# Modulation columns split into four spreads, memory rows turned at the stage border, exponentials issued ahead of the next high part

## The reference

```python
for l in range(DEPTH):                                   # DEPTH = 2
    mod = (cond @ w_mod[l] + b_mod[l])[:, None, :]       # 1024 -> 6 x 1024
    sh_a, sc_a, g_a, sh_f, sc_f, g_f = jnp.split(mod, 6, axis=-1)
    h = rms_norm(x, norm_mix[l]) * (1 + sc_a) + sh_a
    proj = h @ w_in[l]                                   # 1024 x 3072
    # 8 heads of softmax attention, 4 pairs of heads whose weights are a0 - lam * a1
    x = x + g_a * (jnp.concatenate([o_m, o_d], axis=-1) @ w_out[l])
    h = rms_norm(x, norm_ffn[l]) * (1 + sc_f) + sh_f
    x = x + g_f * ((jax.nn.silu(h @ w_gate[l]) * (h @ w_up[l])) @ w_down[l])
```

## Time and profile before

| what | value |
|---|---|
| median of 3 runs | 2824.2 us (2821.93 to 2825.02) |
| the profiled execution, its own time | 2823.45 us |
| its span, first to last instruction | 2821.7 us |
| PE busy | 2741.2 us (97%) |
| DVE busy | 2107.9 us (75%) |
| ACT busy | 1391.6 us (49%) |
| DMA | 537 MB, mean 190 GB/s |
| mean granted TensorE clock | 0.991 |

### The profile page before, as it was taken

How to read it: one execution, slowest core, us unless ns; L and a number is a source line. 1 busy time by engine, 2 the same in 40 slices (tenths; PEclk the granted TensorE clock), 3 DMA queues, 4 the chain that set the end, 5 groups by cost and what they waited for, 6 DMA issues and landing times.

```text
span 2821.7 us, 39962 instructions
## 1 busy us (share of the span) xinstructions
PE 2741.2 (97%) x16410; PEld 2339.2 (83%) x16410; DVE 2107.9 (75%) x3118; ACT 1391.6 (49%) x1630; POOL 208.1 (7%) x172
## 2 busy tenths in 40 slices
PE   8989998999999999999999999999999999999998
PEld 7768887788888788888888888897888888888887
DVE  7777865765555579999879955546699988799655
ACT  4545445554456455554444344465555544444443
POOL 0200001000013001110000000030011100000000
PEclk9999999999999999999999999999999999999999
DMA  8757853655553355554455555633455554454554
GB/s 331 285 216 280 317 187 134 217 194 193 194 200 135 134 179 180 194 179 166 165 176 187 174 194 194 229 135 134 166 178 194 181 174 169 164 194 168 192 194 142
DMA packets 75637, 537.41 MB, mean 190 GB/s; under 512 B 8512, under 2 KB 8896, under 8 KB 12096
## 3 DMA queue, kind: packets, MB, share of 16 engines
q1 hardware_dynamic: 75456, 534.86, 54.1%
HBM read 527.48 MB, written 7.34 MB: 190 GB/s over the span
## 4 chain that ended last, share of the span: by engine, by line
PE 65%; issue 22%; DVE 7%; ACT 4%; DMA 1%; POOL 1%; SPq 0%; DVEq 0%; POOLq 0%; ACTq 0%
PE banks L447 18%; PE banks L455 9%; PE banks L525 7%; PE banks L527 7%; PE banks L535 7%; DVE wlo L1524 3%; PE banks L499 3%; PE banks L501 2%; PE banks L510 2%; ACT whi L1019 2%; PE banks L469 1%; PE banks L471 1%; PE banks L481 1%; PE banks L964 1%; DMA raw<-in_win 1%
## 5 line engine op out<-in xcount | busy, mean ns | idle before, releaser
L1019 ACT ACTIVATE whi<-raw 128x2048 fp32r<-128x2048 f32 x438 | 838.8, 1916 | 990.4 <-issue 799.2
L1524 DVE TENSOR_TENSOR wlo<-raw,whi 128x2048 fp32r<-128x2048 f32 x438 | 1011.9, 2311 | 306.7 <-ACT whi L1019 306.4
L447 PE MATMUL banks<-ht,whi 128*128 128x512 f32 x2880 | 703.1, 393 | 5.9 <-DVE big L1609 2.9
L447 PEld LDWEIGHTS banks<-ht,whi 128*128 128x128 f32 x2880 | 526.5, 188 | 110.1 <-issue 3.7
L525 PE MATMUL banks<-whi,ht 128*128 128x512 f32 x1152 | 456.9, 397 | 13.0 <-DVE ht L1599 9.0
L527 PE MATMUL banks<-whi,ht 128*128 128x512 f32 x1152 | 450.4, 391 | 0.0
L455 PEld LDWEIGHTS banks<-ht,wlo 128*128 128x128 f32 x2880 | 369.1, 191 | 14.6
L455 PE MATMUL banks<-ht,wlo 128*128 128x256 f32 x2880 | 373.4, 283 | 0.0
L535 PE MATMUL banks<-wlo,ht 128*128 128x512 f32 x1152 | 287.4, 389 | 0.0
L525 PEld LDWEIGHTS banks<-whi,ht 128*128 128x128 f32 x1152 | 217.0, 188 | 58.4 <-issue 14.6
L535 PEld LDWEIGHTS banks<-wlo,ht 128*128 128x128 f32 x1152 | 216.2, 188 | 44.9
(11 more groups left out here) (279 smaller groups left out, 3357.5 us busy)
## 6 DMA issues: line engine op xcount, KB each, us to landing
raw<-in_pu SPq DMA_DIRECT2D x128, 1024.0 KB, 4.9
raw<-in_pv SPq DMA_DIRECT2D x128, 1024.0 KB, 4.9
raw<-in_win SPq DMA_DIRECT2D x52, 1024.0 KB, 4.9
big<-in_wmod SPq DMA_DIRECT2D x24, 1024.0 KB, 6.4
raw<-in_wmod SPq DMA_DIRECT2D x24, 1024.0 KB, 5.2
raw<-in_wgate SPq DMA_DIRECT2D x22, 1024.0 KB, 4.9
raw<-in_wup SPq DMA_DIRECT2D x22, 1024.0 KB, 5.1
raw<-in_wdown SPq DMA_DIRECT2D x22, 1024.0 KB, 4.9
```

The source lines that it names most:

```text
L447: m = e.matmul(bank[b + n], h[:, q, c[n]], M.both[:, q * 512:(q + 1) * 512], start=q == 0, stop=False, skip_group_check=True)
L1019: e.activation(whi(j), slot[u][0], ACT.Copy).then_inc(*hi.mark(j))
L1524: e.tensor_tensor(wlo(j), slot[u][0], whi(j).bitcast(F32), ALU.subtract).then_inc(*lo.mark(j))
```

## The change

1. The third chunk of the modulation's columns (parts `sc_f` and `g_f`) is cut in two: `(l, 2)` is `sc_f`, `(l, 3)` is `g_f`. A unit of them still has 1 MB, but holds two groups of 128 rows by 1024 columns, and VectorE works through it in two instructions of 1024 columns, the second behind a wait for the first. Four units make a part.
2. The orders in `lists`: mixer 0 now has twelve modulation units instead of sixteen, never two in a row; `(0, 3)`'s four move to the side slots in feed-forward 0, which then has twenty; mixer 1 keeps eight and starts them earlier.
3. `gate_row` leaves the borders of the stages: gate 0 of layer 1 moves from ahead of mixer 1 to its output projection (where layer 0 already has it), gate 1 of both layers moves from ahead of the feed-forward to after its gate and up units of i = 7.
4. In mixer 1 the four turns of the memory rows move from after unit 4 to ahead of the stage, in the place of `gate_row` and `warm`. ScalarE and VectorE take them over in the steps 0 to 2, two at a time.
5. In ScalarE's loop of both mixers `take` moves behind `score`. `head_squares` moves from step 14 to 13, and `head_sums` of step 14 moves ahead of VectorE's `take`.

```diff
     def munits(l, c):
-        return [("m", a["wmod"][l, c, k], l, c, k) for k in range(8)]
+        return [("m", a["wmod"][l, c, k], l, c, k) for k in range(8)] if c < 2 else [
+            ("m", a["wmod2"][l, c - 2, j], l, c, j) for j in range(4)]
...
-    units += first_mixer(0, [0, 1, 3, 4, 6, 7, 9, 10, 11, 12, 12, 13, 13, 14, 14, 15], munits(0, 1) + munits(0, 2))
-    units += ffn[0][0:1] + spread(ffn[0][1:], munits(1, 0) + munits(1, 1))
-    units += first_mixer(1, [3, 8, 11, 12, 13, 14, 15, 21], munits(1, 2)) + ffn[1]
+    units += first_mixer(0, [0, 1, 2, 3, 5, 7, 9, 11, 13, 15, 16, 17], munits(0, 1) + munits(0, 2))
+    units += ffn[0][0:1] + spread(ffn[0][1:], munits(0, 3) + munits(1, 0) + munits(1, 1))
+    units += first_mixer(1, [1, 4, 7, 10, 13, 16, 18, 20], munits(1, 2) + munits(1, 3)) + ffn[1]
...
# TensorE, first_mixer(1): the start, and after unit 4
-                gate_row(1, 0, (0, 1))
-                warm(name, 6)
+                for t in range(2):
+                    on.wait_ge(*d_mem[t].at(l))
+                for q in range(4):
+                    turn(("m", l), q, MEM, DG[1], q)
                 turn_all(name, XA, DG[0])
...
-                if l and j == 4:
-                    for t in range(2):
-                        on.wait_ge(*d_mem[t].at(l))
-                    for q in range(4):
-                        turn(("m", l), q, MEM, DG[1], q)
...
# TensorE, project and feed_forward
-                    if stage == ("mix1", 0):
-                        gate_row(0, 0, (4, 5))
+                    if stage[0] == "mix1":
+                        gate_row(stage[1], 0, (4, 5))
...
-            gate_row(l, 1, (0, 1))
             warm(name, 6)
...
+                if i == 7:
+                    b = banks.where["g", l, i]
+                    gate_row(l, 1, (b, b + 1))
...
# ScalarE, first_mixer
             for j in range(last + 1):
-                k = take()
                 if 8 <= j < 12:
                     score(2 * (j - 8))
                     score(2 * (j - 8) + 1)
                 if 12 <= j < 16:
                     score(j - 4)
-                if l and j == 5:
-                    for q in range(4):
+                k = take()
+                if l and j < 2:
+                    for q in (2 * j, 2 * j + 1):
                         turn_scaled(("m", l, q), COLS[:, l * 64 + 48:l * 64 + 56], MT, since)
...
-                if j == 14:
+                if j == 13:
                     head_squares(("o1", l, 0), [o[:, 0:512] for o in os], [TMP[:, 0:512], TMP[:, 512:1024]],
...
# VectorE, modulate
+            part(MACC[l, c], r[:, 0:1024], 2 * k, (l, c, k, "first"))
+            on.wait_ge(*mac.at((l, c, k, "first")))
+            part(MACC[l, c], r[:, 1024:2048], 2 * k + 1, (l, c, k))
...
# VectorE, first_mixer
+                if j == 14:
+                    head_sums(("o1", l, 0), [TMP[:, 0:512], TMP[:, 512:1024]], 8, 64, 168)
                 take()
...
-                if l and j == 5:
-                    for q in range(4):
+                if l and j in (1, 2):
+                    for q in (2 * j - 2, 2 * j - 1):
                         rest(("m", l, q), COLS[:, l * 64 + 48:l * 64 + 56], MT)
...
                 if j == 14:
-                    head_sums(("o1", l, 0), [TMP[:, 0:512], TMP[:, 512:1024]], 8, 64, 168)
                     head_scale(("o1", l, 0), [o[:, 0:512] for o in os], 8, 64, 168)
```

53 lines of the change are left out of this document (31 added, 22 removed).

## The result

The changed kernel takes **2816.36 us** in the median of 7 runs (2812.43 to 2820.18), the kernel before 2825.02 in the same comparison (2821.93 to 2826.01). The ratio is 0.9973 with a 95% interval of 0.9961 to 0.9985: faster, by 8.7 us between the medians. The forecast was 2808, that is 16.2 us under the median of before that it went by (2824.2). Nearly half of that gain did not come.

What follows compares the result with a forecast made beforehand. TensorE bounds feed-forward 0, so the gain lies in its waits in the mixers: -8.5 (mixer 0) - 14.4 (mixer 1) + 5.1 (gate rows) + 1.6 (starts) = -16.2 us, giving 2808 us, range 2802 to 2813; 2801 to 2819 with rivals.

Steps and rivals of the forecast that it cites:

- the step on the loop between VectorE and ScalarE: Both mixers: a turn of 7.0 us against TensorE's 8.1 holds TensorE only behind rope; 2.8 us and 1.2 + 1.2.
- what the order was good for: Mixer 0: waits of 15.0 us go, among them exponentials 4.5 and query copy 3.9, with slow stretches of 4.2.
- The memory rows: Mixer 1: turning 3.73 us leaves the path; the 7.27 us wait and a 2.5 us slow stretch go, -13.5.
- The gate rows: Three of them leave idle time for busy time, 1.71 us each, +5.1 us in all.
- The low parts in feed-forward 0: Four more modulation units there add 10 us to VectorE's 164.8 in 214; TensorE stays the bound.
- The halved units: Modulation in two instructions of 1024 columns: at most 0.3 us more per unit, 4 us in all, nothing on the path.
- The wait at win 3: Start of mixer 0: a load taking 7.2 us makes the high part late and TensorE waits 2.1 us.
- The end of mixer 0: Last combine and turned heads 3.2 us, a copy 0.5, projection units 0.4 and 1.7: 5.8, bounds 0 and 8.
- The feed-forward starts: At two starts the wait grows from about 1.0 to 2.7 us; the clock may fall, 1.6 taken, bounds 0 and 3.2.
- The rivals: Waits return, 2819 (0.17); better, 2801 to 2804 (0.10); ScalarE bound, 2834 (0.05); mixer 0 waits stay, 2821 (0.06).
- (a): Rival: the high part behind the exponentials is late in every step, mixer 0 gains nothing net; 2819 us, chance 0.17.
- (c): Rival: ScalarE becomes the bound, each of sixteen steps holds TensorE 1.97 us, +31.5; 2834 us, chance 0.05.

Runs made afterwards that it cites:

- e2: The changed kernel with the high part ahead of the exponentials in every step again, as in the kernel before; 2803.28 us, ratio 0.9920.
- e3: The kernel before with ScalarE's new order alone, head_squares and head_sums moved earlier too, nothing spread or moved besides; 2829.19 us, ratio 1.0012.

## Why the prediction was wrong, step by step

**What failed: the step on the loop between VectorE and ScalarE.** The prediction saw the loop (maxima, exponentials, high part, low part, next maxima) and let it cost nothing as long as its turn of 7.0 us was under TensorE's 8.1. It charged the new order 2.8 us in mixer 0, for a late copy of turned weights and a late query copy in steps 10 and 11, and 2.4 in mixer 1. Neither copy made TensorE wait there: in the changed kernel it has no wait from 124.14 to 170.19, nor from 488.33 to 543.75. What came instead was the wait of unit 10 for banks 2 and 3 in both mixers, and the order cost 13.1 us (2816.36 against 2803.28), 7.9 more than the 5.2 charged; the medians fall short of the forecast by 7.5. Without the 5.2 the sum is -21.4, and the run without the new order gives -22.3.

Two things are wrong in that step.

First, the comparison. In the kernel before the high part was made while ScalarE had nothing else to do, and the low part stood in VectorE's idle time. The turn had not existed so far, and it fits into TensorE's step only if it starts as soon as the scores are there. With the sums behind the low part of step 8, which the prediction did count (7.0 and 1.4 against 8.1), it was already too long, and the exponentials of step 9 came at 117.24, where the version with the high part first has them at 114.48.

Second, the list of what stands behind the high part on ScalarE. The prediction followed the copies of turned weights and the query copy, and not `projected`, which stands right behind them in the same queue and has to empty banks 2 and 3 for the next unit. In the kernel before ScalarE idled 1.31 us ahead of that copy, the copy ended at 123.95 and TensorE started unit 10 at 124.10. So the queue could take some 1.5 us more ahead of the copy before TensorE would feel it, and the high part alone is 1.92; no row of TensorE's waits shows such a slack.

Its price in the changed kernel, by stage and against e2: 3.7 us in mixer 0 (2.45 from unit 9 to unit 10, the rest at the end of the stage), 8.1 in mixer 1 (2.6 from unit 9 to unit 10, 4.4 by slow matmuls in unit 10, 1.15 in the late steps). That the waits themselves (2.54 and 2.70 us) are near the forecast 2.8 and 2.4 is luck, since they stand at another place for another cause; the 4.4 us of slow matmuls were not in the forecast at all.

**Also wrong: what the order was good for.** I gave it the 4.5 us of exponentials in mixer 0 and part of the query copy and the turned weights. The spreading alone takes these of mixer 0 away but for 0.6 us of the weights' copy. "Why the exponentials come late shows on ScalarE" was read rightly from the earlier trace rows (a late load, then a high part, then the exponentials), and then the change was credited with both cures for one illness, one of which has a price.

**Right in size.** The memory rows: 13.5 forecast, 13.4 measured. The gate rows: 1.71 each forecast, 1.74 in feed-forward 0 and 1.71 in the projection of mixer 1 measured. The low parts in feed-forward 0 stay hidden. The halved units: two instructions of 1284 ns are 2.57 against 2.35, 0.22 for the forecast of at most 0.3 (the first figure behind the bar is the busy time, the second the mean ns of one):

```profile
L1555 DVE SCALAR_TENSOR_TENSOR big<-raw,small,big 128x1024 f32<-128x1024 f32 x21 | 27.0, 1284 | 0.4
```

**Right in place, wrong in size.** The wait at win 3 came, with 0.94 us instead of 2.1 in this execution and 0.5 to 1.9 in the other kernels with this order. The load took longer than the row that I used, though, not the usual 4.9:

```profile
DMA to landing us min/median/max: 7.8/7.9/8.1
```

These are the two loads behind the scratch write here, against 7.2 before; TensorE itself came later, after a fall of the clock. The 4.4 us estimated for the megabyte from the Trainium skill (DMA: Bandwidth & Descriptors, Anatomy of one DMA) are further off still. The Trainium skill gives that fit for DMAs that GpSimd issues; in this trace SyncE issues the loads.

The end of mixer 0 was put at 5.8 with a bound of 8. The five waits there sum to 8.4, above that bound:

```profile
175.21 0.49 PE L654 MATMUL banks<-big 128*128 128x128 f32 x2 [0.34 <-ACT big L1150]
179.72 0.52 PE L642 MATMUL banks<-small,big 128*128 128x128 f32 x3 [3.15 <-DVE ht L1614]
180.81 0.79 PE L654 MATMUL banks<-big 128*128 128x128 f32 x2 [0.57 <-ACT big L1150]
193.43 2.11 PE L538 MATMUL banks<-wlo,ht 128*128 128x512 f32 x8 [1.26 <-DVE wlo L1526]
201.18 0.77 PE L528 MATMUL banks<-whi,ht 128*128 128x512 f32 x1 [3.04 <-ACT whi L1021]
```

The second had been put at 3.2 and the last at 1.7. The last is the third projection unit's slot, freed late by the last modulation units, 1.3 us more than forecast.

The feed-forward starts: the wait grew from 1.0 to 2.7 as forecast. A fall makes the turning 5.47 us long instead of 3.84 and the start 1.5 us longer, and it came at both, where I had put 1.6 for the two together.

**The signs.** Of the signs that the prediction named, these came: no wait behind the memory rows and full clock in the step after them, no wait of ScalarE's high part for a wkv load above 3 us in mixer 0, 2.7 us of idle time at the starts. The wait at win 3 is half of what it should be, and TensorE's waits in mixer 0, from its first matmul to 208 us, sum to 12.1 where 10 were expected; 2.54 of them are the wait that was not foreseen. The shortfall of 2.6 us in mixer 0 adds up so: the wait of unit 10 took 0.3 less than the 2.8 charged and win 3 1.2 less than forecast, the fall of the clock at the first unit 1.6 more, and the end of the stage 2.6 more, of which 1.2 are the new order's by the comparison above. The 2.9 in mixer 1 are 5.7 more for the order (8.1 against 2.4), less the 1.6 of the clock at the first unit and less 1.3 for an end of the stage that won more than forecast.

**The rest of the span.** Of the 6.8 us there, 1.7 are the gate row and 1.5 the start of feed-forward 1; the others are falls of the clock in the second stack, which the change does not touch: four in this execution, one in that of before, about 1.2 us each. They follow waits that both kernels have. At the same place, the changed kernel first:

```profile
1432.04 0.47 PE L528 MATMUL banks<-whi,ht 128*128 128x512 f32 x1 [2.00 <-DVE ht L1619]
```

```profile
1433.00:1436.40 3.40, 3.40 (x9) 2.67 (x9) 3.40 (x9) 0.16 (x1) 0.00 (x0) 0.50 0.00 0
```

and the kernel before, 9.8 us later, after the same 2.00 us of idle time:

```profile
1441.87 0.47 PE L525 MATMUL banks<-whi,ht 128*128 128x512 f32 x1 [2.00 <-DVE ht L1604]
```

```profile
1442.00:1446.00 4.00, 4.00 (x18) 3.29 (x19) 4.00 (x10) 0.78 (x2) 0.00 (x0) 1.00 0.00 0
```

So the profiled execution makes the shortfall look larger (10.6 us) than the medians do (16.2 less 8.7, that is 7.5).

**The rivals.** None of the four is what happened. (a) gave a time near the measured one (2819, by high parts that are late in every step), by luck, since its reason does not hold: TensorE waited for a bank in one step of each mixer. (c), ScalarE as the bound, has the right engine; its condition, a turn plus the work between above 8.1 us in most steps, was met in one step of each mixer (9), not in most. What was missing is a rival in which a copy out of PSUM, last in ScalarE's queue, holds a bank.

## What to carry to other kernels

Before moving an instruction back in an engine's queue, list everything that now comes later because of it, down to the last instruction of the step, and for each its slack: the idle time ahead of it in its own queue, and the time from its end to the start of whoever needs it. Here these were 1.31 and 0.15 us against 1.92 put ahead, and the second is in no list of waits. Where two edits cure the same wait, price each as if the other were already made: here the second cost 13 us. Look at which of the two removes the cause (the late load) before paying for the one that works around it.

## What the runs showed of the hardware that I had not expected

A wait of 2.7 us is not followed by half clock each time, and the same wait in the same program can go either way: at the start of mixer 1 every trace has the wait of 2.48 us of the earlier trace rows, and in 8 of 13 the clock fell behind it, in 5 not. Behind the shortest such waits of a start (1.0 us or less) it never fell. What decides between the two for 2.0 to 2.7 us is open. The runs of one kernel differ by 3 to 8 us, which would be two to five falls of 1.5 us; that falls make this scatter is not shown fall by fall, but the run of 2812.43 us of the changed kernel has a mean granted clock of 0.993, and those of 2819.87 and 2820.18 have 0.989.

A wait's length does not tell how long the clock stays down either: behind the bank wait of 2.70 us in mixer 1 it stayed at 0.50 for 10.2 us, in the changed kernel and in e3 alike, though TensorE was busy for 9.37 of the 10.20 us; behind the wait of 2.71 us at the start of feed-forward 0 it was back within 3.5. The first cost 4.4 us. In the kernel before the clock also stood at 0.50 from 461.2 to 471.2, in and behind the 7.27 us wait of the earlier trace rows, but there TensorE was busy in only 4.8 of these 10.0 us, so the slow matmuls cost about 2.4 (an estimate, half of the busy time).
